# Root and reciprocal of six norms on 128x2, spread over the partitions by a product with a diagonal matrix

## The chip, the cores and the metric

The kernel runs on one core of one Trainium2 chip. The metric is the device time of one launch in microseconds. TensorE is PE in the rows (its weight loads are PEld), VectorE is DVE, ScalarE is ACT, GpSimd is POOL, SyncE is SP.

## What is computed

Two stacked networks of two layers each on 256 tokens of 1024 features, in float32. The first has token mixing (a gated recurrence and a latent attention) and a mixture of 16 experts; the second has a window attention, a short convolution, and two feed-forward blocks with convolutions. Ahead of every one of these parts stands a norm with a modulation:

```python
def rmsnorm(x, g):
    xf = x.astype(jnp.float32)
    y = xf * lax.rsqrt(jnp.mean(xf * xf, axis=-1, keepdims=True) + EPS)
    return (y * g.astype(jnp.float32)).astype(x.dtype)
# modulated: y * (1 + scale) + shift, the scale and the shift one number per feature
```

The mean goes over the 1024 features of one token, so the root and the reciprocal are needed once per token: 256 numbers.

## The kernel before

Activations lie with features on the partitions: X and H are 8 tiles of 128 features by 256 tokens (`KT = 8`, `S = 256`). Weights pass through a ring of six buffers that SP fills; PE counts a buffer as free by `multiplied`. Each engine runs its own list of instructions in order, and all order between the engines is written out by hand with semaphores. PE's products are all issued at L400.

A norm has a number n. Norms 0 to 3 belong to the two layers of the first network (n = 2l ahead of the token mixing, n = 2l+1 ahead of the router of the experts), 4 and 5 to the window attention (its own tokens and the context), 6 and 8 to the two feed-forward blocks, 7 to the short convolution. A norm runs like this:

1. DVE adds the last projection to X, tile by tile (L1672 at norm 2, L1687 at norms 1, 3, 6 and 8, L2221 at norm 7), and counts `x_done`.
2. ACT squares each tile into H (L1184) and counts `squares_ready`.
3. At norms 1, 3, 6, 7, 8 (`FOLDED`) DVE adds the squares of tiles 0 to 6 into one (L1679, L2199) and counts `folded`. PE multiplies a 128x128 matrix of ones with this sum and with the square of tile 7, both as 256 moving columns; at norms 0, 2 and 4 there are eight such products, one for each tile as its square comes. The result holds the sum of squares of each token on every one of the 128 partitions, so 128 equal rows of 256.
4. ACT takes the root of it, 128x256, into RST (L1188). DVE takes the reciprocal in place (L1639).
5. DVE multiplies each tile of X with it into H (L1646, eight tiles); ACT scales and shifts six of the tiles (L1193), DVE two of them (L1650). PE's next product waits for the first shifted tile, and takes the others as they come.

At norm 0 PE has other work during the norm. The first products after norms 1 and 3 are those of the router (weights WR, 32 columns), then transposes. `turn_modulation` are sixteen small products for a modulation (128x32 weights, 128 moving columns) ahead of the first weights of norm 6's block. One product in float32 is two matmul instructions and two weight loads in the trace. PSUM is four pairs of banks, PA to PD; the sums of squares lie in PD, at norms 2, 4 and 7 in PA, at norm 5 in PB.

Of the kernel before, what the change touches and what calls it, by code (L numbers as in the profile page):

```python
# [19 lines left out]
ALU = mybir.AluOpType  # L20
# [3 lines left out]
P = 128  # L24
D = 1024
KT = D // P
S = 256
# [92 lines left out]
def stack_program(nc, T, out):  # L120
    ctx = ExitStack()
    with ctx:
        def sb(name, shape, dt=F32):
            return ctx.enter_context(nc.sbuf_tensor(name, shape, dt))

        def sem(name):
            return ctx.enter_context(nc.semaphore(name))
# [13 lines left out]
        RST = sb("RST", [P, 512])  # L141
        LB = sb("LB", [P, 2, 2, 4])
        SM = sb("SM", [P, 220])
        EPSC = sb("EPSC", [P, 1])
        WARM = sb("WARM", [P, 10])
        pair = [ctx.enter_context(nc.psum_tensor(f"pair{i}", [P, 1024], F32)) for i in range(4)]
        PA, PB, PC, PD = [q[:, :] for q in pair]

# [3 lines left out]
        ident, ones = CS[:, C_ID:C_ID + P], CS[:, C_ONE:C_ONE + P]  # L152
# [36 lines left out]
        def state(c, h):  # L189

            if c < 2:
                return F[2][:, 512 * c + h * P:512 * c + h * P + P]
            return F[1][:, 256 + 256 * (h // 2) + h * P:256 + 256 * (h // 2) + h * P + P]
# [53 lines left out]
        def sum_bank(n):  # L247

            return PA if n in (2, 4, 7) else (PB if n == 5 else PD)

        def n_sums(n):

            return n + 1 + (n >= 5)

        FOLDED = (1, 3, 6, 7, 8)

        names = """multiplied const1_in tables_in second_in vec_in x_in pos_in out_stored
        dve_step
        cact_ready rows_summed mod_taken coef_ready rope_ready lb_ready angle_ready
        cz_ready row_ready squares_ready folded sums_ready std_ready scaled_ready h_act h_dve x_done out_tile ctx_squares  # L260
        hf_sig hq_silu v_copied hg_silu lat1_copied lat2_copied gates_act gates_sig filled fill_out
        lat_sums lat_std latn_ready f_ready lnf_ready eb_ready qb_ready kdiff_ready kexp_ready kd_ready
        kd_turned kdt_ready u_ready dec_ready states_ready
# [12 lines left out]
        s = {n: sem(n) for n in names}  # L276
# [3 lines left out]
        def ck(name, l):  # L280
            return CHUNK_OF[name, l]
# [110 lines left out]
        def _(pe):  # L392
# [6 lines left out]
            def mm(o, lhsT, rhs, start, stop, **kw):  # L399
                return pe.matmul(o, lhsT, rhs, start=start, stop=stop, **kw)  # L400
# [52 lines left out]
            def done(last):  # L453
                last.then_inc(s["multiplied"], 1)

            def sums(n, Q):

                if n in FOLDED:
                    pe.wait_ge(s["folded"], FOLDED.index(n) + 1)
                    mm(sum_bank(n)[:, 0:S], ones, Q[:, 0, :], True, False)  # L460
                for t in (7,) if n in FOLDED else range(KT):
                    pe.wait_ge(s["squares_ready"], 8 * n + t + 1)
                    last = mm(sum_bank(n)[:, 0:S], ones, Q[:, t, :], t == 0, t == KT - 1)
                last.then_inc(s["sums_ready"], 1)
# [8 lines left out]
            for l in range(DEPTH):  # L473
# [20 lines left out]
                for m in range(2):  # L494
                    if m:
                        pe.wait_ge(s["mod_taken"], ADA_NO[BEFORE["hi", l][-1]] + 1)
                    for t in range(KT):
                        last = mm(PC[:, 512 * m:512 * m + 512], H1[:, t, m * P:m * P + P], w[:, t, :], t == 0, t == KT - 1)
# [12 lines left out]
                for t in range(KT):  # L511
                    last = mm(PB[64:96, 512:512 + S], w[:, t, P:160], hk(t), t == 0, t == KT - 1)
# [11 lines left out]
                for t in range(3, 5):  # L524
                    last = mm(PD[:, 512:512 + S], ones, sq[:, t, :], t == 3, t == 4)
# [27 lines left out]
                for m in range(8):  # L553
                    last = pe.transpose(PA[:, m * P:m * P + P], KD[:, m * P:m * P + P], ident)
# [23 lines left out]
                for c in range(3):  # L578
                    lo = 64 * (c % 2)
                    for h in range(4):  # L580
                        o = (PA[:, 512 * c:512 * c + 512] if c < 2 else PC[:, 0:512])[:, h * P:h * P + P]
                        last = mm(o, KDT[lo:lo + 64, (2 * h + c // 2) * P:(2 * h + c // 2) * P + P],
                                  VT[lo:lo + 64, 512 * (c // 2) + h * P:512 * (c // 2) + h * P + P], True, True)
# [9 lines left out]
                for h in range(4):  # L593
# [3 lines left out]
                    for c in range(1, 4):  # L597
                        last = mm(PA[:, h * S + c * CH:h * S + c * CH + CH], state(c - 1, h),
                                  QB[:, h * S + c * CH:h * S + c * CH + CH], False, c == 3, skip_group_check=True)
# [8 lines left out]
                for h in range(8):  # L608
                    o = (PC if h < 4 else PD)[0:DQK, (h % 4) * S:(h % 4) * S + S]
                    for t in range(3):  # L610
                        last = mm(o, w[:, t, h * DQK:h * DQK + DQK], CL[:, t, :], t == 0, t == 2)
# [3 lines left out]
                for m in range(2):  # L615
                    last = mm(PB[:, 512 * m:512 * m + 512], ones, F[2][:, 512 * m:512 * m + 512], True, True)
# [4 lines left out]
                for h in range(8):  # L621
# [5 lines left out]
                    for t in range(2):  # L627
                        last = mm(o, w[:, t, h * P:h * P + NOPE], CL[:, 3 + t, :], t == 0, t == 1)
# [4 lines left out]
                for q, a in ((PD, 0), (PA, 1024)):  # L633
                    for m in range(2):
                        last = mm(q[64:96, 512 * m:512 * m + 512], rot, QH[64:96, a + 512 * m:a + 512 * m + 512], True, True)
                    last.then_inc(s["q_turned"], 1)
                wv = w.rearrange("p t (h d) -> p t h d", d=P)
                for m in range(2):
                    for t in range(2):
                        last = mm(PC[:, 512 * m:512 * m + 512], CL[:, 3 + t, m * P:m * P + P],  # L640
                                  wv[:, t, :, NOPE:P], t == 0, t == 1)
# [87 lines left out]
                n = 2 * l + 1  # L729
                sums(n, H1)  # L730
                pe.wait_ge(s["tables_in"], 48)
                for t in range(KT):
                    h_tile(n, t)
                    j = 32 * (t % 4)
                    last = mm(PD[j:j + 32, 512:512 + S], WR[:, t, :], H1[:, t, :], t < 4, t >= 4)
# [11 lines left out]
                for m in range(2):  # L747
                    last = mm(PD[:, 768 + NE * m:768 + NE * m + NE], LOGIT[:, m * P:m * P + P], GATHER[:, :], True, True)
# [43 lines left out]
                def xbank(t):  # L792
                    return pair[t // 2][:, 512 * (t % 2):512 * (t % 2) + 512]

                pe.wait_ge(s["ht_ready"], 2 * l + 2)
                for m in range(2):
                    pe.wait_ge(s["perm_ready"], 2 * l + m + 1)
                    for t in range(KT):
                        last = mm(xbank(t)[:, HALF * m:HALF * m + HALF], HT8[m][:, t, :], PERM[m], True, True)
# [6 lines left out]
                with pe.If(overflow):  # L806
# [4 lines left out]
                    for t in range(KT):  # L811
                        for m in range(2):
                            last = pe.transpose((PA, PB)[t // 4][:, S * (t % 4) + P * m:S * (t % 4) + P * m + P],
                                                HT8[m][:, t, :], ident)
# [21 lines left out]
                with pe.Else():  # L836
# [48 lines left out]
                    for k in range(4):  # L885
                        last = pe.transpose(PC[:, P * k:P * k + P], PLACED[k // 2][:, k % 2 * P:k % 2 * P + P], ident)
# [55 lines left out]
            for t in range(KT):  # L942
                last = mm(PA[:, 512:512 + S], ones, CTXQ[:, t, :], t == 0, t == KT - 1)
# [13 lines left out]
            def wq_tile(c, q, m, first=None):  # L957
                w = view(c, KT, 512)
                for t in range(KT):
                    if first is not None:  # L960
                        h_tile(first, t)
                    last = mm(half(q, m), w[:, t, m * P:m * P + P], H2[:, t, 0:S], t == 0, t == KT - 1)
                return last
# [27 lines left out]
            for m in range(4):  # L991
                last = wq_tile(ck("wqkv", 0), PA, m, 5 if m == 0 else None)
# [20 lines left out]
            for g in range(4):  # L1013
                sel = CS[:, C1_OVER + D_SEL + P * (g % 2):C1_OVER + D_SEL + P * (g % 2) + P]
                o = (PA, PC)[g // 2][:, 512 * (g % 2):512 * (g % 2) + 512]
                last = mm(o, sel, QT[1][:, 512 * (g // 2):512 * (g // 2) + 512], True, True)
# [145 lines left out]
        def _(act):  # L1162
# [13 lines left out]
            def squares(n, X, Q):  # L1176

                A(WARM[:, n:n + 1], EPSC[:, 0:1], ACT.Sqrt)
                for t in range(KT):
                    if n == 0:  # L1180
                        act.wait_ge(s["x_in"], 16)
                    else:
                        act.wait_ge(s["x_done"], 8 * (n - 1) + t + 1)
                    A(Q[:, t, :], X[:, t, :], ACT.Square).then_inc(s["squares_ready"], 1)  # L1184

            def std(n, o, q):
                act.wait_ge(s["sums_ready"], n_sums(n))
                A(o, q, ACT.Sqrt, scale=1.0 / D, bias=EPSC[:, 0:1]).then_inc(s["std_ready"], 1)  # L1188
# [6 lines left out]

            def norm(n, X, H, a, l, which):
                squares(n, X, H)
                std(n, RST[:, 0:S], sum_bank(n)[:, 0:S])
                if n == 0:
                    row_copies()  # L1200
                shifted(n, H, a, l, which)
# [258 lines left out]
            for u in range(16):  # L1460
# [5 lines left out]
                if u % 2 == 0 and u:  # L1466
                    t = u // 2 - 1
# [46 lines left out]
        def _(dve):  # L1514
# [17 lines left out]
            V = dve  # L1532
# [104 lines left out]
            def inverse(n, r):  # L1637
                V.wait_ge(s["std_ready"], n)
                link(V.reciprocal(r, r))  # L1639

            def scaled(n, X, H, r, a, l, which, w=0):

                base = 8 * (h_before(n) + w)

                def tile(t):
                    V.tensor_tensor(H[:, t, :], X[:, t, :], r, ALU.mult).then_inc(s["scaled_ready"], 1)  # L1646

                def shift(t):
                    V.wait_ge(s["scaled_ready"], base + t + 1)
                    V.tensor_scalar(H[:, t, :], H[:, t, :], COEF[:, a, l, which, t, w:w + 1],  # L1650
                                    MOD[:, a, l, 24 * which + t, w:w + 1], ALU.mult, ALU.add).then_inc(s["h_dve"], 1)
                for t in range(5):
                    tile(t)
                if n:
                    shift(3)
                for t in range(5, 8):
                    tile(t)
                if n == 0:
                    first_modulation()
                    shift(3)  # L1660
                shift(7)

            def norm(n, X, H, a, l, which):
                inverse(n_sums(n), RST[:, 0:S])
                scaled(n, X, H, RST[:, 0:S], a, l, which)

            def sorted_residual(X, q, a, l, col, arrived):

# [438 lines left out]
            for i in range(3):  # L2107
                gcol, std = (V_WQ, V_WK, V_WQ)[i], blk(10 + i % 2)
# [5 lines left out]
                n = 2 if i == 1 else 4  # L2114
# [327 lines left out]
```

## Time and profile before

| | us |
|---|---|
| median of 3 runs | 1925.41 |
| lowest and highest | 1923.14, 1927.06 |
| profiled execution | 1920.22 |
| its span | 1918.4 |
| PE busy | 1802.7 (94%) |
| weight loads busy | 1566.8 (82%) |
| DVE busy | 926.4 (48%) |
| ACT busy | 371.9 (19%) |

The profile is one execution. The chain of waits is followed back from the last instruction to what released it. A timeline row merges neighbouring instructions of a kind: start, length, engine, line, and in brackets how long the engine had been idle and what ended that. The granted clock of TensorE is given as a share of 2.4 GHz, 0.50 being 1.2 GHz.

### The profile page before, as it was taken

How to read it: one execution, taken by the hardware profiler on the slowest of the kernel's cores; microseconds unless marked ns; L12 is line 12 of the kernel's file. 1: busy time of each engine (PE TensorE's matmuls, PEld its weight loads, DVE VectorE, ACT ScalarE, POOL GpSimd, SP SyncE). 2: the span in 40 equal slices, each digit the busy share in tenths (PEclk: the TensorE clock that was granted, in tenths of full speed). 3: DMA queues.
4: the chain of work that ended last, by engine and by line, in shares of the span. 5: the costliest groups of instructions: out<-in, count | busy, mean ns of one | idle time of the engine just before them, and what ended most of it. 6: DMA issues, size and time to landing. Idle time of an engine off the chain costs nothing.

```text
span 1918.4 us, 46239 instructions
## 1 busy us (share of the span) xinstructions
PE 1802.7 (94%) x21052; PEld 1566.8 (82%) x21052; DVE 926.4 (48%) x1652; ACT 371.9 (19%) x723; POOL 25.1 (1%) x24
## 2 busy tenths in 40 slices
PE   5899987999998999997999998998999989999999
PEld 3678766899997688676899996657888988878899
DVE  4887877200004868765000004685677651233355
ACT  3013242100002022332000013273111110021110
POOL 0000200000000000200000000000000000000000
PEclk8999999999999999998999999999999999999999
DMA  9995447699996682643999994113887543434330
GB/s 359 387 386 201 177 174 310 235 392 423 422 413 220 233 316 82 220 176 140 374 402 423 421 401 161 46 43 104 291 302 264 208 171 132 159 122 158 131 111 24
DMA packets 180604, 465.90 MB, mean 243 GB/s; under 512 B 5152, under 2 KB 55936, under 8 KB 172288
## 3 DMA queue, kind: packets, MB, share of 16 engines
q1 hardware_dynamic: 180192, 463.83, 64.6%
q8 instruction: 96, 1.57, 0.3%
q10 hardware_dynamic: 288, 0.26, 0.0%
q14 instruction: 28, 0.23, 0.0%
HBM read 463.03 MB, written 1.05 MB: 242 GB/s over the span
## 4 chain that ended last, share of the span: by engine, by line
PE 81%; DVE 12%; DMA 3%; ACT 2%; issue 2%; SPq 0%; ACTq 0%; DVEq 0%
PE pair L400 79%; DMA ring<-in_ada_w 3%; DVE AR L1577 2%; DVE XH L1577 2%; PE pair L1046 1%; DVE RST L1639 1%; DVE AR L1823 1%; ACT AR L1292 1%; DVE AR L1833 0%; SPq L291 0%; PE pair L904 0%; DVE AR L1837 0%; DVE XH L1824 0%; DVE AR L1877 0%; DVE AR L1815 0%
## 5 line engine op out<-in xcount | busy, mean ns | idle before, releaser
L400 PE MATMUL pair<-XH,ring 128*128 128x256 f32 (+1 forms) x3328 | 749.5, 386 | 22.4 <-ACT XH L1193 17.2
L400 PEld LDWEIGHTS pair<-XH,ring 128*128 128x128 f32 (+1 forms) x3328 | 628.1, 190 | 133.2 <-issue 39.8
L400 PE MATMUL pair<-AR,ring 128*64 128x88 f32 (+2 forms) x14336 | 696.8, 249 | 15.4 <-issue 9.1
L400 PEld LDWEIGHTS pair<-AR,ring 128*64 128x64 f32 (+1 forms) x14336 | 667.9, 139 | 38.7 <-issue 18.6
L2076 DVE TENSOR_TENSOR AR<-AR,pair 128x352 f32<-128x352 f32 x32 | 16.7, 521 | 397.5 <-PE pair L400 397.5
L1577 DVE SCALAR_TENSOR_TENSOR AR<-ring,CACT,AR 128x512 f32<-128x512 f32 x245 | 184.2, 752 | 8.7
L400 PE MATMUL pair<-AR 128*64 128x128 f32 (+3 forms) x1600 | 132.0, 292 | 10.2 <-ACT AR L1464 3.3
L400 PEld LDWEIGHTS pair<-AR 128*64 128x64 f32 (+3 forms) x1600 | 106.2, 146 | 19.8 <-issue 6.2
L2282 DVE SCALAR_TENSOR_TENSOR AR<-pair,VEC,AR 128x255 f32<-128x255 f32 x88 | 41.9, 476 | 96.3 <-ACT AR L1489 96.3
L1396 ACT ACTIVATE AR<-pair 128x352 f32 (+1 forms) x64 | 26.4, 465 | 300.9 <-PE pair L400 300.9
L1489 ACT ACTIVATE AR<-pair,VEC 128x256 f32<-128x256 f32 x88 | 36.6, 466 | 214.3 <-PE pair L400 214.3
L1577 DVE SCALAR_TENSOR_TENSOR XH<-ring,CACT,XH 128x512 f32<-128x512 f32 x91 | 74.2, 815 | 3.2
L400 PE MATMUL pair<-ring,XH 128*128 128x512 f32 (+2 forms) x208 | 63.3, 602 | 7.6 <-DMA ring<-in_ada_w 7.6
L1184 ACT ACTIVATE XH<-XH 128x256 f32<-128x256 f32 x64 | 24.3, 412 | 204.0 <-DVE XH L1687 141.7
L400 PE MATMUL pair<-AR,CS 128*32 128x128 f32 (+3 forms) x412 | 49.2, 334 | 12.2 <-DVE AR L1577 10.8
L400 PEld LDWEIGHTS pair<-ring,XH 128*128 128x128 f32 (+1 forms) x208 | 30.1, 176 | 36.1 <-issue 25.5
L400 PEld LDWEIGHTS pair<-AR,CS 128*32 128x32 f32 (+2 forms) x412 | 24.8, 127 | 38.4 <-issue 23.0
L1590 DVE STREAM_TRANSPOSE RST<-pair 128x128 f32<-128x128 f32 x52 | 16.0, 313 | 75.6 <-PE pair L400 74.4
L400 PE MATMUL pair<-XH,CS 128*32 128x128 f32 (+2 forms) x184 | 30.0, 360 | 19.0 <-ACT XH L1184 11.7
L2284 DVE SCALAR_TENSOR_TENSOR AR<-pair,VEC,AR 128x255 f32<-128x255 f32 x88 | 42.5, 483 | 3.1
L400 PEld LDWEIGHTS pair<-XH,CS 128*32 128x32 f32 (+1 forms) x184 | 18.2, 153 | 28.8 <-issue 15.5
L1388 ACT ACTIVATE AR<-pair 128x352 f32<-128x352 f32 x32 | 14.9, 464 | 128.3 <-PE pair L400 128.3
(270 smaller groups left out, 1110.8 us busy)
## 6 DMA issues: line engine op xcount, KB each, us to landing
ring<-in_ada_w SPq DMA_DIRECT2D x48, 2048.0 KB, 13.8
ring<-in_w_gate SPq DMA_DIRECT2D x32, 2048.0 KB, 11.0
ring<-in_w_up SPq DMA_DIRECT2D x32, 2048.0 KB, 11.0
ring<-in_w_down SPq DMA_DIRECT2D x32, 2048.0 KB, 11.6
ring<-in_ffn_w_up SPq DMA_DIRECT2D x44, 1024.0 KB, 7.6
ring<-in_w_in SPq DMA_DIRECT2D x18, 2048.0 KB, 15.9
ring<-in_ffn_w_down SPq DMA_DIRECT2D x8, 2048.0 KB, 8.0
ring<-in_sc_w_in SPq DMA_DIRECT2D x6, 2048.0 KB, 8.1
```

Of the source, the lines that this page charges most:

```text
L400: return pe.matmul(o, lhsT, rhs, start=start, stop=stop, **kw)
L1046: last = pe.transpose(PC[:, m * P:m * P + P], pr[:, m * P:m * P + P], ident)
L1184: A(Q[:, t, :], X[:, t, :], ACT.Square).then_inc(s["squares_ready"], 1)
L1292: ins = A(pr[:, h * nk:h * nk + nk], o[:, h * nk:h * nk + nk], ACT.Exp, scale=float(DQK ** -0.5), bias=NM[u % 2][:, h:h + 1], accum_out=RS ...
L1396: A(YS[:, :, b, bass.ds(first[b], WB)].rearrange("p (k t) n -> p k t n", k=2), PB.rearrange("p (k n) -> p k n", k=2)[:, :, 0:4 * WIN] .rea ...
L1489: A(tmp[:, h, 0:N], bank(b0 + h)[:, 0:N], ACT.Copy, scale=w1).then_inc(s["cv_mid"], 1)
L1577: ins = V.scalar_tensor_tensor(acc, w[:, t, :], cs, acc, ALU.mult, ALU.add)
L1639: link(V.reciprocal(r, r))
L1823: V.tensor_tensor((blk(5), blk(7))[n % 2], blk(0), EE, ALU.mult)
L2076: V.tensor_tensor(HEC[e % 2], SGC, PA[:, 512:512 + 4 * WIN], ALU.mult).then_inc(s["he_ready"], 1)
L2282: link(V.scalar_tensor_tensor(t3[:, :, 1:S], x3[:, :, 0:S - 1], VEC[:, wc:wc + 1], t3[:, :, 1:S], ALU.mult, ALU.add))
L2284: V.scalar_tensor_tensor(t3[:, :, 0:S - 1], x3[:, :, 1:S], VEC[:, wc + 88:wc + 89], t3[:, :, 0:S - 1], ALU.mult, ALU.add).then_inc(s["cv_c ...
```

## The change

At norms 1, 2, 3, 6, 7 and 8 (`COMPACT`) the squares become the weights of the sums, and a single column of ones is the moving operand: for each half of the tokens (128) and each tile one product that leaves the sums of 128 tokens on 128 partitions, in one column of PSUM. The result is 128x2. All squares must be there before the first of these products; norm 2 has sixteen of them, the other five have four. Root and reciprocal are taken on 128x2 (in two new columns of WARM). DVE then multiplies the identity with these two columns into a 128x256 matrix of two diagonals (RDIAG, in RST), and PE multiplies the matrix of ones with it, which puts the 256 reciprocals on every partition of a PSUM bank. The scaled tiles read their factor from there instead of from RST. There are two new semaphores, `rdiag_ready` (DVE to PE) and `spread_ready` (PE to DVE). Norms 0, 4 and 5 stay as they are.

```diff
+        COMPACT = (1, 2, 3, 6, 7, 8)
+        RDIAG = RST[:, 0:S]
+        def spread_over(n):
+            if n in (1, 3):
+                return PA[:, 0:S]
+            return PD[:, S:2 * S] if n in (6, 8) else PD[:, 0:S]
...
+            def compact_sums(n, Q):
+                ts = (0, 7) if n in FOLDED else range(KT)
+                if n in FOLDED:
+                    pe.wait_ge(s["folded"], FOLDED.index(n) + 1)
+                pe.wait_ge(s["squares_ready"], 8 * n + 8)
+                for b in range(2):
+                    for t in ts:
+                        last = mm(sum_bank(n)[:, b:b + 1], Q[:, t, b * P:b * P + P], ones[:, 0:1], t == 0, t == KT - 1)
+                last.then_inc(s["sums_ready"], 1)
+                pe.wait_ge(s["rdiag_ready"], COMPACT.index(n) + 1)
+                mm(spread_over(n), ones, RDIAG, True, True).then_inc(s["spread_ready"], 1)
...
             def sums(n, Q):
+                if n in COMPACT:
+                    return compact_sums(n, Q)
...
                 squares(n, X, H)
-                std(n, RST[:, 0:S], sum_bank(n)[:, 0:S])
+                if n in COMPACT:
+                    std(n, STD, sum_bank(n)[:, 0:2])
+                else:
+                    std(n, RST[:, 0:S], sum_bank(n)[:, 0:S])
...
             def norm(n, X, H, a, l, which):
-                inverse(n_sums(n), RST[:, 0:S])
-                scaled(n, X, H, RST[:, 0:S], a, l, which)
+                if n not in COMPACT:
+                    inverse(n_sums(n), RST[:, 0:S])
+                    return scaled(n, X, H, RST[:, 0:S], a, l, which)
+                inverse(n_sums(n), STD)
+                V.tensor_tensor(RDIAG.rearrange("p (b n) -> p b n", b=2),
+                                ident.rearrange("p (a n) -> p a n", a=1).to_broadcast([P, 2, P]),
+                                STD.rearrange("p (b a) -> p b a", a=1).to_broadcast([P, 2, P]), ALU.mult)\
+                    .then_inc(s["rdiag_ready"], 1)
+                V.wait_ge(s["spread_ready"], COMPACT.index(n) + 1)
+                scaled(n, X, H, spread_over(n), a, l, which)
```

## Rows read from the trace of the kernel before

**Rows 1.** The page: PE's busy time, and the chain that ended last, by engine.

```profile
PE 1802.7 (94%) x21052; PEld 1566.8 (82%) x21052; DVE 926.4 (48%) x1652; ACT 371.9 (19%) x723; POOL 25.1 (1%) x24
...
PE 81%; DVE 12%; DMA 3%; ACT 2%; issue 2%; SPq 0%; ACTq 0%; DVEq 0%
```

**Rows 2.** Chain of waits at norm 1 (start us, us, what), then timeline rows.

```profile
320.54 0.42 ACT XH L1184
320.97 0.04 issue
321.01 0.71 PE pair L400 x2
321.72 0.02 issue
321.75 0.48 ACT RST L1188
322.23 0.02 issue
322.25 1.76 DVE RST L1639
324.02 0.02 issue
324.04 0.44 DVE XH L1646
324.48 0.03 issue
324.50 0.61 ACT XH L1193
...
319.82 0.59 PE L400 MATMUL pair<-XH,CS 128*128 128x256 f32 x2
```

**Rows 3.** Timeline of norm 2: the squares, the eight products of the sums.

```profile
599.56 3.36 ACT L1184 ACTIVATE XH<-XH 128x256 f32<-128x256 f32 x8 [0.47 <-DVE XH L1672]
605.23 0.47 ACT L1188 ACTIVATE RST<-pair,EPSC 128x256 f32<-128x256 f32 x1 [2.32 <-PE pair L400]
...
601.48 3.72 PE L400 MATMUL pair<-XH,CS 128*128 128x256 f32 x16
```

**Rows 4.** Timeline of norm 7: the products of the sums.

```profile
1567.28 1.13 PE L400 MATMUL pair<-XH,CS 128*128 128x256 f32 x4 [1.49 <-DVE XH L2199]
```

**Rows 5.** Windows at the six norms: window, PE, PEld, DVE, ACT, POOL busy; granted clock, DMA share, GB/s.

```profile
325.50:328.50 3.00, 3.00 (x16) 0.96 (x14) 2.05 (x6) 2.98 (x6) 0.00 (x0) 0.50 0.60 239
...
608.70:611.60 2.90, 2.87 (x7) 2.36 (x8) 2.70 (x8) 2.88 (x6) 0.00 (x0) 0.50 0.00 0
...
882.10:884.90 2.80, 2.80 (x14) 1.09 (x16) 2.28 (x7) 2.78 (x6) 0.00 (x0) 0.50 0.55 231
...
1339.10:1342.20 3.10, 3.10 (x8) 2.48 (x9) 2.89 (x11) 2.21 (x5) 0.00 (x0) 0.50 1.06 380
...
1572.00:1577.70 5.70, 5.70 (x14) 4.53 (x15) 2.25 (x7) 2.29 (x5) 0.00 (x0) 0.50 0.19 71
1578.10:1583.10 5.00, 5.00 (x25) 4.41 (x24) 0.00 (x0) 0.00 (x0) 0.00 (x0) 1.00 0.00 0
...
1692.60:1697.30 4.70, 4.70 (x11) 3.75 (x12) 2.22 (x7) 2.26 (x5) 0.00 (x0) 0.50 0.52 165
```

**Rows 6.** Groups by line and form: busy us, mean ns; at L1336 min/median/max ns.

```profile
L1188 ACT ACTIVATE RST<-pair,EPSC 128x256 f32<-128x256 f32 x9 | 4.3, 475 | 14.5 <-PE pair L400 14.5
...
L1336 ACT ACTIVATE SM<-pair x2: 198/198/198, 330.3 to 886.9; 128x32 f32<-128x32 f32 x2
...
L1639 DVE RECIPROCAL RST<-RST 128x256 f32<-128x256 f32 x10 | 17.5, 1752 | 24.9 <-ACT RST L1188 24.9
...
L2143 DVE RECIPROCAL SM<-SM 128x2 f32<-128x2 f32 x16 | 2.7, 166 | 0.5
...
L1646 DVE TENSOR_TENSOR XH<-XH,RST 128x256 f32<-128x256 f32 x72 | 25.6, 420 | 0.3
...
L2076 DVE TENSOR_TENSOR AR<-AR,pair 128x352 f32<-128x352 f32 x32 | 16.7, 521 | 397.5 <-PE pair L400 397.5
...
L1814 DVE TENSOR_TENSOR AR<-AR 128x512 f32<-128x512 f32 x12 | 8.3, 690 | 0.3
```

**Rows 7.** Timeline of the router: products with 16 and with 32 moving columns.

```profile
329.58 0.54 PEld L400 LDWEIGHTS pair<-GATHER,AR 128*128 128x128 f32 x4
...
890.69 0.60 PE L400 MATMUL pair<-SM,CS 128*128 128x32 f32 x4 [2.83 <-DVE SM L1973]
```

**Rows 8.** Clock around gaps of PE (router, softmax), and PE's timeline at softmax, norm 6.

```profile
889.50:891.40 1.90, 0.60 (x4) 0.52 (x4) 1.63 (x10) 0.00 (x0) 0.00 (x0) 1.00 0.00 0
892.00:894.80 2.80, 0.27 (x1) 0.30 (x2) 2.52 (x13) 0.00 (x0) 0.00 (x0) 0.50 0.00 0
...
1249.00:1251.00 2.00, 0.03 (x1) 0.00 (x0) 1.79 (x6) 1.56 (x6) 0.00 (x0) 1.00 1.05 409
1251.20:1253.20 2.00, 2.00 (x14) 1.10 (x14) 1.83 (x4) 1.30 (x5) 0.00 (x0) 1.00 0.52 190
...
1251.03 1.13 PE L400 MATMUL pair<-AR 64*128 64x512 f32 x4 [2.01 <-ACT SM L1455]
...
1335.36 0.64 PE L400 MATMUL pair<-AR,CS 128*32 128x128 f32 x16
1338.97 0.77 PE L400 MATMUL pair<-XH,ring 128*128 128x256 f32 x1 [2.96 <-ACT XH L1193]
```

**Rows 9.** Weight loads of 128x128 at granted clock 0.50 (1572 to 1577.7) and 1.00.

```profile
L400 PEld LDWEIGHTS pair<-XH,ring 128*128 128x128 f32 x15 | 4.8, 331 | 5.1 <-issue 3.9
...
L400 PEld LDWEIGHTS pair<-XH,ring 128*128 128x128 f32 x29 | 5.5, 190 | 0.7
```

More of the change, by code:

```diff
@@ L144, in stack_program @@
         EPSC = sb("EPSC", [P, 1])
-        WARM = sb("WARM", [P, 10])
+        WARM = sb("WARM", [P, 12])
+        STD = WARM[:, 10:12]
         pair = [ctx.enter_context(nc.psum_tensor(f"pair{i}", [P, 1024], F32)) for i in range(4)]
@@ L259, in stack_program @@
         cact_ready rows_summed mod_taken coef_ready rope_ready lb_ready angle_ready
-        cz_ready row_ready squares_ready folded sums_ready std_ready scaled_ready h_act h_dve x_done out_tile ctx_squares
+        rdiag_ready spread_ready cz_ready row_ready squares_ready folded sums_ready std_ready scaled_ready h_act h_dve x_done out_tile ctx_squares
         hf_sig hq_silu v_copied hg_silu lat1_copied lat2_copied gates_act gates_sig filled fill_out
```

## The prediction

> **What bounds the kernel now.** I read the page first: PE is busy for 94% of the span and PE holds 81% of the chain that ended last [rows 1]. So DVE or ACT matter only where PE stands still for them, and the norms are such places: each of the six that the change touches has a reciprocal of 128x256 on that chain. Then I read the chain of waits around the second norm of layer 0 (norm 1 in the code) [rows 2]. After the last square (ended 320.96) come the last product of the sums (0.71 us), the root (0.48), the reciprocal (1.76), the first scaled tile (0.44) and its shift on ACT (0.61); only then does PE go on. Between the square's end and the first tile lie 3.08 us, between the last product and the next one 3.53 us in which PE does nothing. Norms 3, 6 and 8 show the same chain. Norm 7 differs ahead of the root: its two products (four instructions, 1.15 us) start together once the last fold is done [rows 4]. Norm 2 has eight products, which PE runs one behind the other beside the squares; the last square ends at 602.91 and the sums at 605.21 [rows 3].
>
> The second thing to see is the granted clock [rows 5]. In each of the six gaps it falls from 1.00 (2.4 GHz) to 0.50 (1.2 GHz) before PE has its first tile or just as it comes, and PE then works 3.0, 2.9, 2.8, 3.1, 5.7 and 4.7 us at half speed: 22.2 us, that is 11.1 us lost, more than all six reciprocals (10.5 us). What the change does to the clock therefore weighs more than the roots it shortens.
>
> **The change, part by part, at full clock.** *Root and reciprocal.* The root falls from 0.475 to about 0.20 (a 128x32 activation from PSUM took 198 ns), the reciprocal from 1.753 to 0.166 (the 128x2 row) [rows 6]. *Added:* one diagonal product on DVE, 128x256 with two broadcast operands: 0.42 by the 128x256 row; I see no reason for another price, bounds 0.41 to 0.48 [rows 6]. Then a product of ones with it on PE, 128x256 from a standing start: 0.71 plus 0.04 until it starts [rows 2]. Hand-overs are 0.02 to 0.04 each [rows 2], and there are two more of them. From the end of the sums to the first tile: before 0.02+0.48+0.02+1.76+0.02 = 2.30; after 0.02+0.20+0.02+0.17+0.03+0.42+0.04+0.71+0.02 = 1.63. That is 0.67 less at each norm. *Tiles from PSUM:* the scaled tiles now read their factor from PSUM. A 128x352 tensor_tensor with a PSUM operand takes 521 ns; between the SBUF rows of 256 (420) and 512 (690) the same size comes to 521. So nothing [rows 6]; at worst 0.06 once a norm, the rest of the tiles being covered by the shifts on ACT, which take longer.
>
> *The sums.* The squares become weights with one moving column. Such pairs (a load of 128x128 and a short matmul) show in the router: two products with 32 moving columns, four pairs, took 0.60 us from a standing start, and four pairs with 16 columns 0.54 for the loads, one every 0.115 us [rows 7]. A folded norm needs two halves times two tiles, four products or eight pairs, and all of them now wait for the last square, since the fold's product is no longer ahead of it: 0.63+4x0.115 = 1.09 against 0.71, 0.38 more. Together with the 0.67 norms 1, 3, 6 and 8 gain 0.29 each, 1.2 us in all. Norm 7 had 1.15 and now has 1.09, counted from the square 0.1 later: it gains 0.6. Norm 2 has 16 products, 32 pairs, none of which may start before 602.91+0.04: 0.63+28x0.115 = 3.85, so its sums end at 606.8 instead of 605.2. It loses 1.6, gets 0.67 back, and is 0.9 slower. Sum at full clock: -1.2-0.6+0.9 = -0.9 us.
>
> *What is queued behind.* In PE's queue the wait for the diagonal stands ahead of the next weights. At norm 6 the 16 turning products (0.64 us, run in the gap now [rows 8]) move behind the spread; they then lie beside the first tile and its shift (1.05 us and the hand-overs), so they cost nothing at full clock, 0.1 at half. On DVE only the tiles stand behind the wait for the spread. No DMA is moved; the ring's next loads wait for later products.
>
> **The clock after the change.** Wide products stop earlier than now: at 319.82 instead of 320.41 before norm 1, 1.15 us ahead of the last square [rows 2], and 1.5 us ahead of it at norm 2. Then come short pairs, 0.9 us of nothing, the spread (0.7), 1.2 us of nothing. The nearest row is the router: after 2.83 us of idleness four short pairs ran, 0.60 us, and the clock stood at 0.50 before PE came back [rows 7, 8]. So work in the middle of a gap need not hold it. Norm 6 says the same: 0.64 us of turning products ahead of 2.96 us of idleness, and it fell as well [rows 5, 8]. I take it that the six cold stretches stay as long as they are. What becomes new is that added PE work itself can meet the low clock. A load of 128x128 took 190 ns at 1.00 and 331 at 0.50 [rows 9]; a 128x256 product is two such pairs, and 14 of them ran in 5.70 us at 0.50 against 25 in 5.00 at 1.00 [rows 5]. The spread would cost 0.4 more; I take half of the norms, 1.2 us (bounds 0 and 2.4). At norm 2 the pairs go on for almost 4 us with no wide product since 601.5; the clock may fall in the midst of them. I take half of the 32 at 0.115 more: 1.8 us (bounds 0 and 3.7). Forecast: -0.9+1.2+1.8 = **+2.1 us**.
>
> In the gap the Trainium skill speaks for the opposite. Its page "TensorE: Matmul & The Clock Gate", section "Why this matters for your kernels", advises against idle gaps of PE between bursts of matmuls, since an idle engine goes back to the low clock; a product placed within the gap would then be worth its time twice. The router's rows do not bear this out, the softmax rows do; by it the sum would be that of the first rival.
>
> **The rivals.** *First: the broken gap keeps the clock.* No stretch of idleness is longer than 1.3 us any more (apart from norm 2, 1.5), where now it is 2.96 to 3.53. For it: in the softmax of the window attention PE stands idle for 2.01 us between products and the clock is 1.00 before and after [rows 8]. It hangs on whether loads with a single moving column count as work, which no row decides. With four of six cold stretches gone: -0.9-7.4 = -8.3 us, 1917; with all of them gone -12 us, 1913.4. *Second, on the slow side: norm 2 goes cold.* Place: the 32 pairs of norm 2. If the low clock comes as they begin, they cost 3.7 more; a clock that falls so early also takes all six spreads (2.4) and keeps PE low for as long after norm 2 as after norm 7, 5.7 us instead of 2.9, 1.4 more: -0.9+3.7+2.4+1.4 = +6.6 us, 1932. From eight cold pairs on (8x0.115 = 0.9) the gain at full clock is used up, and the sign turns. *Third: it does not do what it says*, the short pairs costing 0.23 each like wide ones (16 in 3.72 us [rows 3]): 8x0.23+0.1 is 0.85 more at each of five norms, 4.2 us, and 32x0.23-3.85 is 3.5 more at norm 2: -0.9+4.2+3.5 = +6.8. The router's rows speak against it; I give it 2 in 100 and count it with the second.
>
> **How the numbers follow.** The profiled execution took 1920.22 us with a span of 1918.4; the three timed runs have a median of 1925.41, 5.2 more, and lie 3.9 apart. The sum made against the profiled one gives 1922.3; carried to the median it is 1927.5. Chances: forecast 0.50, first rival 0.31, second (with the third) 0.19. A measurement of this kernel can tell 0.2%, 3.9 us. The forecast's own bounds are -0.9 and +5.2, so I put 0.40 of its 0.50 within the band, 0.08 above and 0.02 below; the first rival gives 0.28 to faster and 0.03 to the band, the second 0.17 to slower and 0.02 to the band. That makes faster 0.30, same 0.45, slower 0.25. The range goes from most of the first rival (1914.5) to a little over the second (1933).
>
> **What the profile will show.** Right: reciprocals of about 0.17 us at six norms; sums of about 1.1 us after the last square (3.9 at norm 2); a tensor_tensor of 0.42 and a product of 0.7 ahead of the first tile; first tile 2.8 us after the last square at full clock; the clock still at 0.50 behind each norm. Wrong: a clock of 1.00 when the first tiles come, which is the first rival; sums at norm 2 of 5 us and more, the second; tiles of over 0.45 us, which would show a price of PSUM that I set at nothing.

## The result and the profile after

| | us |
|---|---|
| median before, 14 runs | 1924.79 (1921.3 to 1929.47) |
| median after, 14 runs | 1928.93 (1923.81 to 1933.16) |
| ratio | 1.0022, 95% interval 1.0012 to 1.0032 |
| profiled execution after, its span | 1929.79, 1928.0 |

The change costs 4.1 us, just over the 0.2% that a measurement of this kernel can tell from no change; the interval reaches from 2.3 to 6.2 us. The forecast was 2.1 us of loss, the range 1914.5 to 1933.

The chain of waits of the changed kernel at norm 1 (start us, us, what) answers to [rows 2]:

```profile
320.00 0.42 ACT XH L1208
320.42 0.14 issue
320.56 1.04 PE pair L409 x8
321.60 0.02 issue
321.62 0.27 ACT WARM L1212
...
321.91 0.18 DVE WARM L1666
...
322.11 0.43 DVE RST L1695
...
322.59 0.71 PE pair L409 x2
...
323.33 0.43 DVE XH L1673
```

Every added piece is there: eight short pairs (1.04), the root on 128x2 (0.27), the reciprocal (0.18), the diagonal (0.43), the spread (0.71). From the last square's end (320.42) to the first tile it takes 2.91 us, where it took 3.08. The lines and forms of the touched instructions, min/median/max in ns, against [rows 6]:

```profile
L1666 DVE RECIPROCAL WARM<-WARM x6: 165/166/166, 321.9 to 1699.2; 128x2 f32<-128x2 f32 x6
...
L1212 ACT ACTIVATE WARM<-pair,EPSC x6: 262/262/263, 321.6 to 1698.9; 128x2 f32<-128x2 f32 x6
...
L1695 DVE TENSOR_TENSOR RST<-CS,WARM x6: 424/425/426, 322.1 to 1699.4; 128x256 f32<-128x256 f32 x6
```

Norm 2 is another matter. First PE's timeline there, then two windows in it (window, PE, PEld, DVE, ACT, POOL busy; granted clock, DMA share, GB/s), against [rows 3] and [rows 5]:

```profile
602.22 5.06 PE L409 MATMUL pair<-CS,XH 128*128 128x1 f32 x32 [1.42 <-ACT XH L1208]
608.28 1.22 PE L409 MATMUL pair<-RST,CS 128*128 128x256 f32 x2 [1.01 <-DVE RST L1695]
610.75 5.60 PE L409 MATMUL pair<-XH,ring 128*128 128x256 f32 x16 [1.24 <-ACT XH L1217]
...
602.50:604.00 1.50, 1.50 (x15) 1.50 (x16) 0.00 (x0) 0.00 (x0) 0.00 (x0) 1.00 0.07 26
604.60:607.20 2.60, 2.60 (x13) 2.59 (x13) 0.00 (x0) 0.00 (x0) 0.00 (x0) 0.50 0.00 0
```

The 32 pairs stand behind the last square (602.17) and take 5.06 us; in their midst the clock falls from 1.00 to 0.50, and the last 13 pairs start 0.213 us apart, where the first ones start 0.112 apart. It fell while PE was busy with nothing but short pairs, and stayed low through the spread (1.22 instead of 0.70) and the first products behind it. From the last square to the first tile it is 7.37 us, where it was 4.61 [rows 3].

The last view is one that the prediction did not use: how long PE waited for nothing that the profile shows ("issue" in the list of waits: sum, times, longest). First the kernel before, then the changed one:

```profile
PE pair L400 <- issue: 10.1, 13, 1.2
```

```profile
PE pair L409 <- issue: 16.0, 16, 2.4
```

All but two waits of 0.5 us in each lie at the loops over the experts, between norms 1 and 2 (3.7 us before, 3.8 after) and between norms 3 and 4 (5.3 before, 11.1 after), where not one instruction was changed.

### The profile page after: what moved, and what is told of

Read it like the earlier page. It is cut to its first block, busy times and chain, and to the rows that moved or that the text cites. A ratio compares the mean times of both kernels' runs of the same rounds, so it can differ in the third digit from the quotient of the medians.

```text
span 1928.0 us, 46346 instructions
## 1 busy us (share of the span) xinstructions
PE 1813.2 (94%) x21100; PEld 1574.5 (82%) x21100; DVE 919.4 (48%) x1658; ACT 370.5 (19%) x723; POOL 24.5 (1%) x24
## 3 DMA queue, kind: packets, MB, share of 16 engines
q8 instruction: 97, 1.59, 0.3%
HBM read 463.03 MB, written 1.05 MB: 241 GB/s over the span
## 4 chain that ended last, share of the span: by engine, by line
PE 81%; DVE 12%; ACT 2%; DMA 2%; issue 2%; SPq 1%; ACTq 0%; DVEq 0%
PE pair L409 80%; DVE AR L1604 2%; DMA ring<-in_ada_w 2%; DVE XH L1604 2%; PE pair L1070 1%; DVE AR L1858 1%; ACT AR L1319 1%; DVE AR L1868 0%; SPq L300 0%; PE pair L928 0%; DVE AR L1872 0%; DVE XH L1859 0%; DVE AR L1912 0%; DVE AR L1850 0%; DVE AR L1859 0%
## 5 line engine op out<-in xcount | busy, mean ns | idle before, releaser
L409 PEld LDWEIGHTS pair<-AR,CS 128*32 128x32 f32 (+2 forms) x412 | 24.8, 127 | 34.7 <-issue 23.3
L1722 DVE SCALAR_TENSOR_TENSOR XH<-pair,MOD,XH 128x256 f32<-128x256 f32 x32 | 14.4, 480 | 41.5 <-PE pair L409 41.4
L409 PE MATMUL pair<-XH,CS 128*32 128x128 f32 (+3 forms) x148 | 19.4, 347 | 15.6 <-ACT XH L1208 9.8
```

## The experiments

Theories once the two traces were compared: A, the loss is norm 2's; B, it is spread over all six norms; C, the low clock behind a norm's gap is what the norms cost most, against D, holding the clock there gains nothing; E, short pairs count as idleness for the clock, against F, they hold it; G, where PE's code lies sets its gaps at the experts, against H, they hang on what PE executes at the norms or vary from one execution to the next. All ratios are to the kernel before, with their 95% intervals.

**Norm 2 put back.**

```diff
-        COMPACT = (1, 2, 3, 6, 7, 8)
+        COMPACT = (1, 3, 6, 7, 8)
```

> The changed kernel with norm 2 put back as it was before (eight wide products beside the squares, root and reciprocal on 128x256); norms 1, 3, 6, 7, 8 stay compact. Theory A (the loss is norm 2's: 32 short pairs after the last square, part of them at the low clock): the five norms gain 0.2 to 0.6 us each at full clock and give some of it back in colder stretches, so about 0 to 2 us under the kernel before, ratio 0.999 to 1.000; from the last square to the first tile 2.85 us at these five. Theory B (the loss is spread over all six norms, by spread products and tiles at the low clock): ratio stays near 1.002.

Measured: 1.0001 (0.9988 to 1.0013). The five norms gain nothing that can be measured; a gain of the size that the chain shows (1.2 us, below) would be lost in this interval.

**Norm 2 alone.**

```diff
-        COMPACT = (1, 2, 3, 6, 7, 8)
+        COMPACT = (2,)
```

> The kernel before with norm 2 alone made compact. Theory A: it carries the whole loss, 3 to 6 us over the kernel before, ratio 1.0015 to 1.003; the sums take 4 to 7 us after the last square, and the granted clock falls to 0.50 while the short pairs run and stays there until wide products have run for a while. Theory B: under 1 us, ratio 1.000 to 1.0005.

Measured: 1.0027 (1.0015 to 1.0038), 5.2 us. Its profile has the 32 pairs at 4.99 us, and the first tile 7.31 us after the last square, 2.7 later than before. So A holds against B: norm 2 alone costs as much as the whole change, the other five together cost nothing that can be measured. The chain at norm 2 shows 2.7 of the 5.2 us; what the rest is, this run doesn't say.

**Norm 2's products as the squares come.**

```diff
+                if n == 2:
+                    for t in ts:
+                        pe.wait_ge(s["squares_ready"], 8 * n + t + 1)
+                        for b in range(2):
+                            last = mm((PA, PB)[b][:, 0:1], Q[:, t, b * P:b * P + P], ones[:, 0:1], t == 0, t == KT - 1)
...
+                    A(STD[:, 0:1], PA[:, 0:1], ACT.Sqrt, scale=1.0 / D, bias=EPSC[:, 0:1])
+                    A(STD[:, 1:2], PB[:, 0:1], ACT.Sqrt, scale=1.0 / D, bias=EPSC[:, 0:1]).then_inc(s["std_ready"], 1)
```

> The changed kernel, but at norm 2 each tile's two short products run as its square comes (one column in each of two PSUM pairs, the root taken in two activations), instead of all sixteen after the last square. Theory A (norm 2's loss is the 32 pairs behind the last square and the low clock within them): the sums end 0.5 to 1.2 us after the last square instead of 5.1, first tile 3 us or so after the last square, norm 2 about 5 us shorter than in the changed kernel, total 0.9985 to 1.000 of the kernel before. Rival: the clock then falls while the pairs trickle, and cold stretches behind norm 2 eat most of it: 1.001 to 1.002.

Measured: 1.0013 (1.0005 to 1.0022), above the 0.9985 to 1.000 expected. I had expected the sums 0.5 to 1.2 us behind the last square. They end 2.3 us behind it (609.38 against 607.08):

```profile
605.65 3.73 PE L409 MATMUL pair<-CS,XH 128*128 128x1 f32 x32
610.54 1.22 PE L409 MATMUL pair<-RST,CS 128*128 128x256 f32 x2 [1.16 <-DVE RST L1708]
```

PE has other products until 605.65, and then 32 pairs take 3.73 us, to a hundredth the 3.72 of the eight wide products before [rows 3]. A pair of a load and one moving column took 0.117 us (3.73 over 32), half of a pair with 256 columns (0.23); halving the tokens per product doubles the number of pairs, and nothing is left of the shorter moving operand. From the last square PE's first product is 5.92 us away (613.00), where it was 5.81 before and 8.57 in the changed kernel: the loss at norm 2's chain is nearly gone. The gain on the whole is argued from the trace: the two intervals, 1.0005 to 1.0022 here and 1.0012 to 1.0032 for the changed kernel, overlap. The ratio lies where the rival had it, and its low clock is part of that: PE works 5.3 us at 0.50 from the spread on, where it was 3.1 before, which is about 1 us lost. The waits for nothing shown are 16.4 us, as long as in the changed kernel.

**A wide filler in the idle gap.** Kernel before, nothing compact; behind the sums of the six norms:

```diff
+        FILLED = {1: 7, 2: 7, 3: 7, 6: 6, 7: 7, 8: 7}
...
+                for _ in range(FILLED.get(n, 0)):
+                    mm(spare_bank(n), ones, CS[:, 0:S], True, True)
```

> The kernel before, nothing compact, but PE runs seven wide products (128x256 moving, six at norm 6) into an unused PSUM bank right behind the sums of norms 1, 2, 3, 6, 7, 8, where it stood idle for 3.5 us; their results are not used. Theory C (the norms' larger cost is the low clock that follows the idle gap, 22.2 us at half speed in the profile of before): the granted clock stays 1.00 at these norms, the first tiles start at the same place, and the kernel is 6 to 11 us under the one before, ratio 0.994 to 0.997. Rival D (the clock after a norm falls for another reason, or PE is then held by the tiles' arrival and not by its own speed): the ratio is 0.999 to 1.001.

**A narrow filler of the same length.**

```diff
+                for _ in range(2 * FILLED.get(n, 0)):
+                    mm(spare_bank(n)[:, 0:1], ident, ones[:, 0:1], True, True)
```

> As the kernel with wide filler products, but each is replaced by two products with the identity as weights and a single moving column (14 products, 28 pairs, about 3.3 us at full clock), so that PE is as long occupied, with weight loads. Theory E (short pairs count as idleness for the clock): the clock falls to 0.50 as in the kernel before or within the pairs, which then take up to twice as long; 0 to 6 us slower than before, ratio 1.000 to 1.003. Rival F (they hold the clock, as my first rival had it): the same gain as the wide filler, ratio 0.994 to 0.997.

Measured: wide 0.9994 (0.9984 to 1.0005); narrow 1.032 (1.030 to 1.034). What the two say of the clock is plain in their windows at norm 1, the filler first, the router's products behind it. Wide:

```profile
321.25 3.19 PE L407 MATMUL pair<-CS 128*128 128x256 f32 x14
324.94 1.34 PE L407 MATMUL pair<-XH,WR 128*32 128x256 f32 x6 [0.51 <-ACT XH L1202]
...
321.30:324.40 3.10, 3.10 (x15) 2.42 (x13) 2.41 (x3) 0.68 (x2) 0.00 (x0) 1.00 0.84 344
325.00:328.00 3.00, 3.00 (x17) 0.90 (x18) 2.24 (x7) 2.98 (x6) 0.00 (x0) 1.00 0.59 226
```

Narrow:

```profile
322.04 3.23 PE L407 MATMUL pair<-CS 128*128 128x1 f32 x28
325.73 1.58 PE L407 MATMUL pair<-XH,WR 128*32 128x256 f32 x6 [0.46 <-ACT XH L1202]
...
322.10:325.00 2.90, 2.90 (x29) 2.90 (x27) 2.22 (x3) 0.49 (x2) 0.00 (x0) 1.00 0.79 306
325.80:328.30 2.50, 2.50 (x14) 1.03 (x16) 2.23 (x7) 2.48 (x6) 0.00 (x0) 0.50 0.67 282
```

PE is occupied for the same 3.2 us, up to 0.5 us before its next product. Behind 14 wide instructions the clock is 1.00, behind 28 pairs of a 128x128 load and one column it is 0.50. E holds of the clock, F falls: in this gap such pairs did no more for it than idleness. The wide filler kept the clock at all six norms; nothing is at 0.50 in its trace between 1566 and 1584, where the kernel before has 5.7 us of it [rows 5].

But the wide filler gained nothing that can be told, where 0.994 to 0.997 was expected, and the narrow one lost 61 us where at most 6 were; the norms hold none of it: from the last square to the tiles it is as fast as the kernel before. The waits for nothing shown, wide and narrow:

```profile
PE pair L407 <- issue: 16.7, 18, 1.8
```

```profile
PE pair L407 <- issue: 61.2, 29, 12.6
```

One of the narrow filler's three long ones, in the second layer's experts:

```profile
1089.62 5.56 PE L407 MATMUL pair<-AR,ring 128*64 128x88 f32 x98 [12.56 <-issue]
```

So added instructions of PE can cost something far from where they stand. In the narrow filler the three long waits (11.6, 12.6 and 11.0 us) are 35 of the 61 us. For the wide one it is a guess so far: its profile is of the fastest of its twelve runs (1916.47, the median 1922.75), so the trace doesn't show where the median run lost its gain.

**The same instructions, ahead of the experts.** Kernel before, all norms untouched:

```diff
                 sums(2 * l, H1)
                 if l == 0:
+                    for _ in range(24):
+                        mm(PC[:, 512:513], ident, ones[:, 0:1], True, True)
```

> The kernel before, all norms as before, with 24 products of the identity with one moving column (48 pairs, about 5.5 us) behind the sums of norm 0, where PE waits about 4 us for the first modulation weights; results unused. It puts as many instructions into PE's stream as the change does, and nothing else. Theory G (where PE's code lies sets how long PE stands still for nothing the profile shows, at the first experts of each layer: 9.6 us before, 15.4 after, 57.7 with the narrow filler): that sum moves to 12 us or more, or well below 9, and the time with it, 2 to 6 us. Rival H (these gaps hang on what PE executes at the norms, or vary from one execution to the next): gaps of 8 to 11 us and a ratio of 0.999 to 1.001.

**The same instructions, behind the experts.** The narrow filler, again 24 products:

```diff
-        FILLED = {1: 7, 2: 7, 3: 7, 6: 6, 7: 7, 8: 7}
+        FILLED = {6: 4, 7: 4, 8: 4}
```

> The kernel before with the same 24 products of one moving column (48 pairs) as in the code shift, but eight in each idle gap of norms 6, 7 and 8, behind both loops over the experts instead of ahead of them. Theory G (PE's code ahead of the loops sets its gaps there): the gaps at the experts stay at 8 to 12 us and the ratio is 0.999 to 1.001. If added instructions cost wherever they stand, it is near the 1.0056 of the code shift.

Measured: ahead 1.0056 (1.0043 to 1.0069), behind 1.0000 (0.9989 to 1.0011). The waits for nothing shown sum to 19.2 us in the first and 11.8 us in the second. G holds: 48 pairs behind both loops cost nothing, the same 48 ahead of them cost 10.8 us, more than the 2 to 6 expected. None of it lies ahead of the experts: the reciprocal of norm 1 starts at 321.60, and at 322.25 in the kernel before. The two versions differ in one more thing, which no run took apart: ahead the pairs stand in one block, behind in three of sixteen.

**The two kernels once more, unaltered.**

> The changed kernel, nothing altered, for a second profile of the same program. Theory G: the gaps of PE at the experts sum to about the 15.4 us of its first profile (14 to 17) and lie at the same places. Rival H: they sum to something else, 9 to 13 us. The loss at norm 2 (5.1 us for the sums, low clock from within them) should come again within 1 us.

> The kernel before, nothing altered, for a second profile. If its gaps of PE at the experts are a property of the program they sum to 9 to 11 us again (9.6 in the first); if they vary from one execution to the next as far as between kernels, to 12 us or more. The low clock follows each of the six norms again, 20 to 26 us of PE's work at half speed there.

The waits for nothing shown are 14.6 us in the changed kernel (16.0 in its first profile) and 12.5 in the kernel before (10.1). They differ by 1.4 and 2.4 us between two executions of one program, and both of the changed kernel are above both of the other. That is weak evidence. Counted as its expectation counts (9.6 in the first profile), the kernel before has 12.0 in the second, where 9 to 11 would have meant a property of the program; and at the second loop the second profiles of the two kernels are alike (8.0 before, 8.2 after).

All profiles together say more. At the first loop the four with no PE instruction added ahead of it (the two of before, norm 2 alone, the shift behind) have 3.0 to 4.6 us of such waits, the others 3.8 to 7.9, most with 48 pairs added. At the second loop the three with nothing added ahead have 5.3 to 8.0, the changed kernel 11.1 and 8.2, the shift ahead 10.3 and the narrow filler, with 84 pairs ahead, 54.3.

PE's work at 0.50 behind the six norms is 22.7 us in the second profile of the kernel before, as expected. At norm 2 the second profile of the changed kernel has all its pairs at 1.00:

```profile
606.97 3.73 PE L409 MATMUL pair<-CS,XH 128*128 128x1 f32 x32 [1.42 <-ACT XH L1208]
611.71 1.22 PE L409 MATMUL pair<-RST,CS 128*128 128x256 f32 x2 [1.01 <-DVE RST L1695]
```

Here the expectation missed: sums of 3.7 us, not 5.1. Whether the clock falls within the pairs or behind them (it's 0.50 from 610.7 on) differs from one execution to the next; from the last square (606.91) to the first tile (612.97) it is 6.06 us here and 7.37 in the first profile. The spread is cold in both.

**A filler of fewer instructions.** As the wide filler, with four products of 448 moving columns (three at norm 6) instead of seven of 256:

```diff
+        FILLED = {1: 4, 2: 4, 3: 4, 6: 3, 7: 4, 8: 4}
...
+                    mm(spare_bank(n).rearrange("p (a n) -> p a n", a=2), ones,
+                       CS[:, 0:224].rearrange("p (a n) -> p a n", a=1).to_broadcast([P, 2, 224]), True, True)
```

> The kernel before with filler products again, but four (three at norm 6) of 448 moving columns instead of seven (six) of 256: about the same time of PE, 46 instructions more than before instead of 82. Theory C and G together: the clock stays at 1.00 at the six norms, 11 to 12 us less at half speed, and less of it is given back in PE's unexplained gaps at the experts than the 16.2 us seen with the 256-column filler; ratio 0.994 to 0.998. Rival D: the ratio is 0.999 to 1.001 whatever the gaps are.

Measured: 0.9978 (0.9969 to 0.9986), the first version that beats the kernel before. Where its gain is and where it goes shows in the stretches between the reciprocals of the norms, worked out from their starts in the traces (us):

| | 1 to 2 | 2 to 3 | 3 to 6 | 6 to 7 | 7 to 8 | 8 to end |
|---|---|---|---|---|---|---|
| before | 283.5 | 273.4 | 456.9 | 233.0 | 120.6 | 228.9 |
| before again | 283.7 | 273.3 | 460.8 | 232.7 | 120.4 | 228.8 |
| longer filler | 284.8 | 271.6 | 463.2 | 231.4 | 117.7 | 226.6 |
| code shift, ahead | 290.5 | 271.8 | 464.0 | 232.8 | 120.5 | 228.9 |
| code shift, behind | 286.7 | 273.0 | 460.1 | 233.0 | 120.6 | 228.9 |

In the four stretches without experts, the second and the last three, the filler gains 1.8, 1.6, 2.9 and 2.3 us, 8.6 us in all; PE's work at 0.50 behind norms 2, 6, 7 and 8 was 17.2 us in the kernel before, half of which is 8.6. C holds for what the clock costs. But the medians show only 0.22%, 4.2 us, so half of the 8.6 or more is given back. In the table it would be in the two stretches with experts (1 to 2, 3 to 6), with a loss of 1.3 and of 2.4 to 6.3 us, but that isn't shown: these stretches vary by as much between profiles with the same code up to there, 283.5 to 286.7 in the first (both of before, shift behind) and 456.9 to 460.8 in the second. That the longer code of PE is what takes it back is argued from the two shifts.

**The filler at norm 5 too.**

```diff
-        FILLED = {1: 4, 2: 4, 3: 4, 6: 3, 7: 4, 8: 4}
+        FILLED = {1: 4, 2: 4, 3: 4, 5: 4, 6: 3, 7: 4, 8: 4}
```

> The kernel before with the 448-column filler of the last experiment at the six norms and also behind the sums of norm 5, where PE stands idle for 3.5 us as well. Theory C: one more cold stretch goes (3.3 us at half speed before, 6.0 with the filler at six norms alone), so 1.5 to 3 us less again: ratio 0.996 to 0.9975. Rival: 0.9978 as before, since the added instructions cost in gaps what the clock gives back.

Measured: 0.9980 (0.9967 to 0.9993), the rival's ratio. The cold stretch behind norm 5 is gone from its trace, and the time is that of the filler at six norms: what this adds is below what can be told, which neither supports nor excludes the 1.5 us.

**Compact chain and filler together.** Norms 1, 3, 6, 7, 8 compact, with a 448-column product in each hole of PE:

```diff
+                if n != 7:
+                    filler(PD[:, 512:960])
                 pe.wait_ge(s["squares_ready"], 8 * n + 8)
...
                 last.then_inc(s["sums_ready"], 1)
+                filler(PD[:, 512:960])
                 pe.wait_ge(s["rdiag_ready"], COMPACT.index(n) + 1)
                 mm(spread_over(n), ones, RDIAG, True, True).then_inc(s["spread_ready"], 1)
+                if n != 6:
+                    filler(PD[:, 512:960])
```

> The changed kernel without norm 2 (norms 1, 3, 6, 7, 8 compact), with one 448-column filler product in each hole of PE that the compact chain leaves (ahead of the last square, behind the sums, behind the spread; fewer at norms 6 and 7), and four at norms 2 and 5. If the compact chain is worth its 0.3 to 0.6 us a norm once the clock is held, this is 1 to 2 us under the filler at seven norms, ratio 0.995 to 0.997. If its holes still let the clock fall at some of the norms, 0.997 to 0.999.

Measured: 0.9972 (0.9958 to 0.9986). The clock is held at all of the norms but norm 7. At norms 1, 3, 6 and 8 the first tile comes 2.85 us after the last square (3.08 before); at norm 7 the spread meets the low clock (1.12 us) and it is 3.44, no gain on the 3.40 before. It beats the kernel before, and cannot be told from the filler alone: the compact chain, at best 1.2 us over five norms, adds nothing that shows.

## Why the prediction came out as it did

**Sum at full clock (-0.9 forecast).** Most pieces were right to a few hundredths: pairs 1.04 (1.09 forecast), reciprocal 0.17, diagonal 0.425 (0.42), spread 0.70, scaled tiles from PSUM 0.41 (no dearer than from SBUF, as argued from the 128x352 row). Two were mis-sized, both upwards: the root on 128x2 takes 0.262, not 0.20 (the 128x32 row was a sigmoid without a bias tile, the root has one; no run separates the two), and PE starts its first pair 0.14 after the square, not 0.04, for which the profile shows no cause. So a folded norm gains 3.08-2.91 = 0.17, not 0.29; norm 7 gains 3.40-2.91 = 0.49, not 0.6; norm 2 loses 6.06-0.52-4.61 = 0.93 with the cold part of its spread taken out, as forecast (0.9). Together -0.68-0.49+0.93 = -0.2.

**Pairs at the low clock (+1.8 forecast, bounds 0 and 3.7).** 5.06-3.73 = 1.3 in one profile (13 pairs, 0.10 more each, where 16 at 0.115 were taken), 0 in the other. The mechanism is as described, and the place; how much of it an execution sees varies, and two profiles don't give its mean. **Spreads at the low clock (+1.2 forecast).** In the first profile those of norms 2 and 8 were cold (1.22 and 1.05 against 0.70): 0.9; in the second norm 2's alone: 0.5. **Cold stretches as long as before.** PE's work at 0.50 at the six norms, added up over windows of a quarter microsecond, is 29.4 us in the first profile of the changed kernel, pairs and spreads among it, and 23.3 in the second, against 23.4 and 22.7 in the two of the kernel before. So the stretches behind the norms stayed near the same in their sum, and the step from the router's row, that work in the middle of a gap need not hold the clock, was right. One by one they did not stay: in the second profile it is 3.1 and 3.4 us behind norms 7 and 8, where the kernel before had 5.9 and 4.8, and 5.6 behind norm 1, where it had 3.3.

**First rival, the broken gap keeps the clock (0.31).** It fell. The trace of the changed kernel has 0.50 behind all six norms, and the narrow filler answers what the prediction left open: 3.2 us of loads with one moving column did not hold the clock. The rival hung on a guess about just this, and the router's row, four short pairs and a clock at 0.50 behind them, already spoke against it; 0.31 was too much. **Second rival, norm 2 goes cold (0.19).** Half of it: the place is the right one and norm 2 alone carries the loss, and the first profile has the sums of over 5 us that were this rival's sign. But a full 6.6 us needs a clock that falls as the pairs begin, which neither profile shows; the second has sums of 3.8 us. **Third, pairs as dear as wide ones:** no, 0.117 us each against 0.23.

**What the sum did not have.** With -0.2 at full clock and 0.5 to 2.2 for cold pairs and spreads, the terms of the forecast as measured give 0.3 to 2.0 us of loss; 4.1 were measured (2.3 to 6.2). The likely missing term is PE's waiting for nothing shown at the experts: 16.0 and 14.6 us against 10.1 and 12.5, 4.0 us more in the mean of two profiles each. That PE's code ahead of the loops can cause it is shown by the two shifts; that it is these 4 us in the changed kernel is argued from four profiles, with 1.4 and 2.4 us between two profiles of one program, and not isolated: norm 2 alone has 12.8, the five others alone 12.1. Against it speaks that norm 2 alone loses 5.2 us with these 12.8. For it speaks the kernel with norm 2's products beside the squares, where the chain's own loss is nearly gone and 0.13% stays, with 16.4 us of such waits. The prediction had these gaps before it on the page ("issue") and passed over them, because nothing there was edited. Its own step "what is queued behind" asked for waits and transfers, not for where the instructions come to lie.

The direction was right, and norm 2's 32 pairs were the right place for the part of it that the sum could know. That 4.1 us lies so near the forecast of 2.1 is in part luck: the chain terms came out between 0.3 and 2.0, and what makes up the rest was not in the sum. Why the waits depend on where PE's code lies stays open. The queue that loads instructions moved 1.57 MB in the kernel before, 1.59 in the changed one and 2.05 in the narrow filler with its 12 us gaps, which points to the loading of code in loops over experts for the narrow filler. For the changed kernel it says little: norm 2 alone and the five others alone moved 1.59 too. No run here separates alignment, length and the loops' own reloads.

## What to carry to other kernels

Turning the operands of a reduction product around, so that the data are the weights, trades moving columns for weight loads. Here a product with one column took 0.233 us (two pairs), one with 256 columns 0.465, and twice as many were needed, so PE's own time is no shorter. What pays is the root and the reciprocal on 128x2, and only where few products stand behind the last square: with four the chain got 0.17 us shorter, with sixteen it got 1.4 to 2.8 us longer. A gap in which PE waits for a chain of small steps costs more than itself when the clock falls in it. Wide products of no use held the clock here, narrow ones did not, and the version with fewer instructions was the one that gained, since code added ahead of a long loop can cost more than it brings. Time such a change with a control that adds the same instructions elsewhere.

## What the runs showed of the hardware

- Clock: at norm 1, 3.2 us of weight loads with single-column products left the clock to fall to 0.50 as it does behind the idle gap of the kernel before; 3.2 us of 256-column products in the same place held it at 1.00. At 0.50 the short pairs started 0.213 us apart, at 1.00 0.112 (changed kernel, norm 2).
- PE's instruction stream: 96 instructions (48 loads, 48 matmuls) ahead of two loops cost 10.8 us, the same number behind them nothing that can be measured, and 164 pairs spread over six norms cost 61 us, some 50 of it as waits of up to 12.6 us at which the profile shows no cause.
- A tensor_tensor of 128x256 with one operand in PSUM took 0.413 us in the mean, with both in SBUF 0.418 (changed kernel).
